# Order and fillers of block 0, and ten weight buffers from slot 22 of block 1, in a two-layer hybrid decoder step

## The chip, the cores and the metric

The kernel runs on one core of a Trainium2 chip. The metric is device time in microseconds, the median of three runs. Each core has a matrix engine (PE, with its weight loads as PEld), a vector engine (DVE), an activation engine (ACT), a general engine (POOL), and SP, which here only issues DMA transfers and waits. Each engine works through its own list of instructions in order, and an instruction may wait for semaphores that other engines or landed transfers raise. ACT issues the weight transfers from its own list; SP issues all others.

## The reference

Two layers over a prompt of 2048 tokens (width 1024) and over eight single decode tokens. Cut to what matters:

```python
h = _rmsnorm(x, norm_w)
z = einsum('btd,dc->btc', h, w_in)          # q,k,v,gate of GLA; 16 low-rank gate inputs; q,k,v,gate of retention
la = log_sigmoid(glr @ gla_w2 + gla_b) / 16
# GLA:       S_t = exp(la_t) S_{t-1} + k_t^T v_t ;  o_t = q_t S_t
# retention: S_t = gamma_h S_{t-1} + k_t^T v_t ;    o_t = q_t S_t   (q, k rotated)
o_a = rms(o_a) * silu(gate_a);  o_b = groupnorm(o_b) * silu(gate_b)
y = x + concat(o_a, o_b) @ w_out            # twice (DEPTH = 2); then a final RMSNorm
```

The outputs are both token streams and, per layer, the recurrent states of the prompt and of the eight decode rows.

## The kernel before, in words

The prompt is cut into four blocks of 512 tokens per layer, so there are eight block passes, n = 0 to 7; n = 0 to 3 are layer 0, n = 4 to 7 layer 1. "Block 0" and "block 1" are the first and second pass of a layer (`kind` 0 and 1). In a pass PE runs 32 slots (w = 1 to 32) and a slot 0. Four slots make a unit u, which fills the four accumulator banks P[0..3] over eight K tiles, two K tiles a slot. A slot holds 24 matmuls of 512 columns: four banks by two K tiles by three products (high by high, low by high, high by low part), since each fp32 operand is split into a high and a low part (`products`, L733). Slot 0 (`hT_slot0`, L700) multiplies the normed activations by the 16 low-rank gate columns; `gate_expand` (L754) turns that into the forget gate.

The weights of a slot are two halves h (512 columns each), 64 halves a pass. For each half ACT issues the load (`load_half`, L258) and makes the high part (`split_hi`, L267); POOL makes the low part (`split_lo`, L274), which PE awaits as `lo_done`. In its turn w, ACT does: split half 2w+2, load half 2w+4, split half 2w+3, load half 2w+5, and only then the copies of that turn. There are ten staging buffers: 0 to 3 are `w_stage`, 4 to 7 lie in `ss` and 8 to 9 in `v_b`. `ss` and `v_b` also hold the decode states and products, which block 1 needs. So `buffer(h)` gives block 1 only buffers 0 to 3 for its first halves, and all ten later. Before a load into a buffer, ACT waits until POOL has split the buffer's last half; where no half has used the buffer within the last ten, it waits for `state_out`: both decode states of the layer stored by SP (`save_states`, L466), and for the decode outputs (`so_ps`). `state_out` is 64 after layer 0 and 128 after layer 1.

SP's list in a pass follows w = 0 to 19. At w = 6 it turns the keys through DRAM (`out_k_rows` L437, `k_n` L442), at w = 16 to 19 of the passes n = 3 to 6 it reads the next block's activations with eight transfers each (`load_next`, L397), and at w = 19 of block 1 it stores the GLA decode state (L466), behind that turn's `load_next`.

At the start (n = 0) DVE computes row statistics, POOL the reciprocal roots, PE turns them into a bank (`scale_rows`, L364), DVE scales the K tiles one after the other (`next_scaled`, L377), ACT makes their high part (`next_hi`, L353), DVE their low part (`next_lo`, L357). Between these DVE works on the decode rows: `sample_stats`, `sample_mean`, `sample_norm`. In block 1, DVE and ACT in slots 20 to 25: `outputs_pair` (L994, L1000) is PE's attention output, ACT copies it (L1189), DVE takes its statistics (L1563), multiplies gates (`silu`, L1592) and normalises (L1586).

Of the kernel before, what the change touches and what calls it, by code (L numbers as in the profile page):

```python
# [25 lines left out]
TOK = 128  # L26
# [34 lines left out]
def build(nc, d):  # L61
# [3 lines left out]
    with ctx:  # L65
# [164 lines left out]
        def buffer(h):  # L230
            return h % HALVES % STAGED if h // HALVES % NBLK == 1 and h % HALVES < 48 else h % STAGES
# [126 lines left out]

        def scale_rows(pe):

            for t in range(TPB):
                if t % 2 == 0:
                    pe.wait_ge(first_rs, t // 2 + 1)
                i = pe.transpose(ATT[:, TOK * t:TOK * t + TOK], xrs[:, t:t + 1].to_broadcast([128, 128]), ident[:, :])  # L364
            i.then_inc(ht_ps.sem, KT)

# [226 lines left out]
        def _(pool):  # L593
# [36 lines left out]
            for h in range(2):  # L630
                split_lo(pool, h)
            pool.wait_ge(s_v.sem, s_v.at(0, V_NV - V_LAST))
            rsqrt(srs[:, :], svar[:, :], s_p.sem)
            for h in range(2, 2 * AHEAD):
                split_lo(pool, h)
# [41 lines left out]
        def _(pe):  # L677
# [10 lines left out]
            for l in range(DEPTH):  # L688
                def body(l, n, kind):
                    def hT_slot0():  # L690
# [11 lines left out]
                        if kind == 0 and n > 0:  # L702
# [55 lines left out]
                    def first_slot():  # L758

                        for k in range(2):  # L760
                            pe.wait_ge(lo_done, k + 1)
                            pe.wait_ge(hlo_sb.sem, hlo_sb.at(0, k + 1))
                            products(0, 0, 0, (k,))
                        for q in range(4):
                            if q > 0:
                                i = products(0, 0, q)
                            if q == 0:
# [3 lines left out]
                    def unit_slot(u, s):  # L771
                        first = n * HALVES + 2 * (4 * u + s)
# [7 lines left out]
                        for q in range(4):  # L780
# [3 lines left out]
                            if n == 0 and u == 0 and s == 1:  # L784
                                if q == 0:
                                    sample_transposed(0)
                                if q == 1:
                                    gate_expand()
                                if q == 2:
                                    sample_gate()  # L790
                            if q < 3 and s == 3:
                                i.then_inc(proj.sem, 1)
                        if kind == 0 and u < 6 and s % 2 == 1:
                            if s == 1:
                                free_sample_bank(u)
# [55 lines left out]
                    def sample_work(w):  # L851
                        if kind == 0:
                            if w == 2:
# [4 lines left out]
                            if w == 6:  # L858
# [157 lines left out]
                    for w in range(1, SLOTS):  # L1016
                        u, s = (w - 1) // 4, (w - 1) % 4
                        if n == 0 and w == 1:
                            first_slot()
                            hT_slot0()  # L1020
# [5 lines left out]
                        if w == 1:  # L1026
                            gate_expand()
                        if kind > 0:
# [27 lines left out]
        def _(act):  # L1056
# [7 lines left out]
            split_hi(act, 0)  # L1064
            split_hi(act, 1)
            load_half(act, 4)
            load_half(act, 5)
            for k in range(KT):
                next_hi(act, 0, k)
                if k in (3, 5):  # L1070
                    split_hi(act, (k + 1) // 2)
            for l in range(DEPTH):
                def body(l, n, kind):
# [11 lines left out]
                    def sample_work(w):  # L1085
# [7 lines left out]
                        if w == 2:  # L1093
# [830 lines left out]
```

## Time and profile before

| | |
|---|---|
| median of 3 runs | 1668.95 us (1668.67 to 1671.54) |
| the profiled execution | 1668.71 us, its span 1666.9 us |
| PE busy | 1641.7 us (98%) |
| DVE, ACT, POOL busy | 1064.9, 618.6, 840.0 us |
| granted clock of TensorE | 0.999 of full speed |

The span runs from the first to the last instruction; 1.8 us of the execution lie outside it. Times in the rows are microseconds from the span's start. A row of the timeline gives start, duration, engine, line of the kernel, operation, names, shape and count, and in brackets the idle time of the engine before it with what ended it. Consecutive matmuls overlap, so the cost of one is read from the distance between two starts, not from its duration.

### The profile page before, as it was taken

What the parts mean: (1) busy time and instruction counts of PE and PEld (TensorE: products, weight loads), DVE (VectorE), ACT (ScalarE), POOL (GpSimd) and SP (SyncE); (2) the same over time, 40 slices, a digit from 0 to 9 for tenths busy, and PEclk for the clock granted to TensorE, in tenths of its full rate; (3) what the DMA queues carried; (4) which work ended last, traced back from release to release, by engine and by line L of the source; (5) the groups of instructions that cost most, each with busy time, mean ns of one, the idle gap of its engine ahead of it and who ended that gap; (6) DMA issues with size and microseconds to landing.
All of it is one profiled execution on the core that took longest, in us unless ns stands there. A gap on an engine that the chain in (4) does not pass through costs nothing.

```text
span 1666.9 us, 26235 instructions
## 1 busy us (share of the span) xinstructions
PE 1641.7 (98%) x9742; PEld 1346.4 (81%) x9742; DVE 1064.9 (64%) x2388; ACT 618.6 (37%) x1166; POOL 840.0 (50%) x645
## 2 busy tenths in 40 slices
PE   6999999999999999999999999999999999999998
PEld 4788878887788887888878888788887888878886
DVE  7743666867765575547855467767787557784474
ACT  4423444243342343423443234342333424442342
POOL 4443645645455464444544445556554555554455
PEclk9999999999999999999999999999999999999999
DMA  7634657656564474467643566567864466553554
GB/s 266 154 109 110 183 203 221 192 155 169 194 177 128 114 208 133 120 151 160 202 134 97 151 143 196 163 172 188 193 193 132 122 163 158 171 173 103 142 155 142
DMA packets 389136, 268.19 MB, mean 161 GB/s; under 512 B 290704, under 2 KB 293136, under 8 KB 389008
## 3 DMA queue, kind: packets, MB, share of 16 engines
q1 hardware_dynamic: 315136, 131.99, 31.6%
q10 hardware_dynamic: 73872, 134.51, 25.6%
q8 instruction: 77, 1.26, 0.3%
q14 instruction: 51, 0.42, 0.1%
HBM read 219.34 MB, written 47.07 MB: 160 GB/s over the span
## 4 chain that ended last, share of the span: by engine, by line
PE 90%; DVE 4%; DMA 2%; issue 1%; SPq 1%; POOL 0%; ACT 0%; ACTq 0%; POOLq 0%; DVEq 0%
PE bank L733 78%; PE bank L994 2%; PE bank L1000 1%; PE bank L978 1%; PE bank L956 1%; PE bank L798 1%; PE bank L935 1%; SPq L442 1%; DMA region<-in_x_prompt 1%; PE bank L700 1%; DMA out_k_rows<-region 1%; DMA w_stage<-in_w_slots 1%; PE bank L939 1%; PE bank L1011 0%; PE bank L808 0%
## 5 line engine op out<-in xcount | busy, mean ns | idle before, releaser
L274 POOL TENSOR_TENSOR w_lo<-w_stage,w_hi 128x512 fp32r<-128x512 f32 x264 | 371.7, 1428 | 331.3 <-ACT w_hi L267 331.2
L733 PE MATMUL bank<-h_hi,w_hi 128*128 128x512 f32 x1024 | 408.3, 399 | 4.1 <-DVE h_lo L357 4.1
L733 PE MATMUL bank<-h_lo,w_hi 128*128 128x512 f32 x1024 | 399.8, 390 | 0.0
L733 PE MATMUL bank<-h_hi,w_lo 128*128 128x512 f32 x1024 | 399.4, 390 | 0.0
L274 POOL TENSOR_TENSOR w_lo<-ss,w_hi 128x512 fp32r<-128x512 f32 x164 | 224.3, 1387 | 211.2 <-ACT w_hi L267 211.1
L267 ACT ACTIVATE w_hi<-w_stage 128x512 fp32r<-128x512 f32 x264 | 153.8, 624 | 369.1 <-PE bank L733 286.8
L733 PEld LDWEIGHTS bank<-h_hi,w_hi 128*128 128x128 f32 x1024 | 192.4, 188 | 55.4 <-issue 8.1
L733 PEld LDWEIGHTS bank<-h_hi,w_lo 128*128 128x128 f32 x1024 | 192.5, 188 | 41.1
L733 PEld LDWEIGHTS bank<-h_lo,w_hi 128*128 128x128 f32 x1024 | 192.7, 188 | 37.2
L733 PE MATMUL bank<-w_hi,m_hi 128*128 128x512 f32 x512 | 200.6, 392 | 2.0 <-DVE region L1592 2.0
L733 PE MATMUL bank<-w_hi,h_hi 128*128 128x512 f32 x512 | 201.1, 393 | 0.0
L733 PE MATMUL bank<-w_lo,h_hi 128*128 128x512 f32 x512 | 199.4, 389 | 0.0
L733 PE MATMUL bank<-w_lo,m_hi 128*128 128x512 f32 x512 | 199.3, 389 | 0.0
L733 PE MATMUL bank<-w_hi,h_lo 128*128 128x512 f32 x512 | 199.2, 389 | 0.0
L733 PE MATMUL bank<-w_hi,m_lo 128*128 128x512 f32 x512 | 199.2, 389 | 0.0
L267 ACT ACTIVATE w_hi<-ss 128x512 fp32r<-128x512 f32 x164 | 95.8, 624 | 232.0 <-PE bank L733 176.6
L274 POOL TENSOR_TENSOR w_lo<-v_b,w_hi 128x512 fp32r<-128x512 f32 x84 | 115.9, 1399 | 116.2 <-ACT w_hi L267 116.0
L607 POOL TENSOR_TENSOR rstd<-var,half 128x4 f32<-128x4 f32 x64 | 66.7, 1042 | 128.9 <-DVE var L1576 68.0
L733 PEld LDWEIGHTS bank<-w_hi,m_hi 128*128 128x128 f32 x512 | 96.1, 188 | 24.2 <-issue 4.3
L733 PEld LDWEIGHTS bank<-w_hi,h_hi 128*128 128x128 f32 x512 | 96.2, 188 | 21.5 <-issue 1.2
L733 PEld LDWEIGHTS bank<-w_hi,m_lo 128*128 128x128 f32 x512 | 96.1, 188 | 20.2
L733 PEld LDWEIGHTS bank<-w_hi,h_lo 128*128 128x128 f32 x512 | 96.1, 188 | 20.2
(218 smaller groups left out, 2209.9 us busy)
## 6 DMA issues: line engine op xcount, KB each, us to landing
w_stage<-in_w_slots ACTq DMA_DIRECT2D x264, 256.0 KB, 3.7
ss<-in_w_slots ACTq DMA_DIRECT2D x164, 256.0 KB, 3.6
v_b<-in_w_slots ACTq DMA_DIRECT2D x84, 256.0 KB, 3.7
region<-in_x_prompt SPq DMA_DIRECT2D x32, 512.0 KB, 5.2
out_o_rows<-region SPq DMA_DIRECT2D x64, 256.0 KB, 3.1
region<-out_o_rows SPq DMA_DIRECT2D x192, 64.0 KB, 3.4
xn<-in_x_t SPq DMA_DIRECT2D x16, 512.0 KB, 5.0
out_k_rows<-region SPq DMA_DIRECT2D x32, 256.0 KB, 3.9
```

The lines of the kernel that those rows point to most:

```text
L267: nc.scalar.activation(w_hi[:, h // 2 % RING, c], stage(h), ACT.Copy).then_inc(hi_done, 1)
L274: pool.tensor_tensor(w_lo[:, r, c], stage(h), w_hi[:, r, c].bitcast(f32), ALU.subtract).then_inc(lo_done, 1)
L442: sp.dma_start(k_n[32 * j:32 * j + 32, t, :].rearrange("p (f a) -> p f a", a=32), runs[t][j]).then_inc(kb_in.sem, 16)
L607: pool.tensor_tensor(dst, src, half[0:dst.shape[0], 0:dst.shape[-1]], ALU.pow).then_inc(s, 1)
L700: i = pe.matmul(ATT[r, 0:256], wg[:, k, :], x_t[:, k, 256 * hf:256 * hf + 256], start=(k < 2), stop=(k >= 6))
L733: i = pe.matmul(P[q][:, :], x, y, start=(s == 0 and kk == 0 and c == 0), stop=(s == 3 and kk == 1 and c == 2), skip_group_check=True)
L798: i = pe.matmul((ST if Z_BANK[u] == "S" else X)[32 * c:32 * c + 32, 0:128], hs[:, k, :], stage(first - 2 * s + k)[:, 128 * c:128 * c + 128 ...
L935: pe.matmul(OUT[hh][:, c], a[:, h, :], v_n[:, t, 128 * h:128 * h + 128], start=(p == 0), stop=False, skip_group_check=True)
L939: i = pe.matmul(OUT[hh][:, c], q_two[g][r, p, tile], s[r, c], start=False, stop=(p == 1), skip_group_check=True)
L956: i = pe.matmul((ST, X)[t // 2][r, c:c + 128], k_n[:, t, 64 * h:64 * h + 64], v_n[:, t, 128 * h:128 * h + 128], start=True, stop=True)
L978: i = pe.matmul(SC_TWO[hh][:, c:c + 128], k_t[r, p, tile], q_two[g][r, p, tile], start=True, stop=True)
L994: pe.matmul(OUT_TWO[hh][:, c:c + 128], a_two[g][:, t % 2, h, :], v_n[:, t, 128 * h:128 * h + 128], start=(t % 2 == 0 and p == 0), stop=Fal ...
```

## The change

In block 0 of the first pass (n = 0): slot 0's low-rank product moves from behind slot 1 to behind slot 2; the decode rows' transposes, gate and gate expansion move later by one place or one slot, and ACT and DVE follow (`late`). `idle_turns` puts 10, 18 and 8 transposes of the identity into an unread bank on PE: between the two pairs of `scale_rows`, behind them, and between the products of the first and the second K tile. `sample_norm` stands two K tiles sooner on DVE. ACT makes the high part of K tile 0 ahead of weight half 1. POOL splits halves 2 and 3 before the decode root. On DVE `queries` is taken out of `rotate`; it stands in front of the second half of the gate. In both layers, block 1 uses all ten buffers from half 42 (slot 22) instead of half 48 (slot 25).

```diff
         def buffer(h):
-            return h % HALVES % STAGED if h // HALVES % NBLK == 1 and h % HALVES < 48 else h % STAGES
+            return h % HALVES % STAGED if h // HALVES % NBLK == 1 and h % HALVES < 42 else h % STAGES
...
+        def idle_turns(pe, count):
+
+            for _ in range(count):
+                pe.transpose(X[:, 0:128], ident[:, :], ident[:, :])
+
         def scale_rows(pe):
             for t in range(TPB):
                 if t % 2 == 0:
+                    if t > 0:
+                        idle_turns(pe, 10)
                     pe.wait_ge(first_rs, t // 2 + 1)
                 i = pe.transpose(ATT[:, TOK * t:TOK * t + TOK], xrs[:, t:t + 1].to_broadcast([128, 128]), ident[:, :])
             i.then_inc(ht_ps.sem, KT)
+            idle_turns(pe, 18)
...
             for h in range(2):
                 split_lo(pool, h)
+            for h in range(2, 2 * AHEAD):
+                split_lo(pool, h)
             pool.wait_ge(s_v.sem, s_v.at(0, V_NV - V_LAST))
             rsqrt(srs[:, :], svar[:, :], s_p.sem)
-            for h in range(2, 2 * AHEAD):
-                split_lo(pool, h)
...
                             products(0, 0, 0, (k,))
+                            if k == 0:
+                                idle_turns(pe, 8)
                         for q in range(4):
                             if q > 0:
                                 i = products(0, 0, q)
-                            if q == 0:
+                            if q == 2:
                                 sample_sum(0)
...
-                            if n == 0 and u == 0 and s == 1:
-                                if q == 0:
-                                    sample_transposed(0)
-                                if q == 1:
-                                    gate_expand()
-                                if q == 2:
-                                    sample_gate()
+                            if n == 0 and w == 2 and q == 2:
+                                sample_transposed(0)
+                            if n == 0 and w == 3 and q == 0:
+                                gate_expand()
...
                             if s == 1:
+                                if u == 0:
+                                    pe.wait_ge(s_v.sem, s_v.at(l, V_H))
                                 free_sample_bank(u)
...
                             first_slot()
-                            hT_slot0()
                             continue
...
+                        if n == 0 and w == 2:
+                            hT_slot0()
...
             split_hi(act, 0)
+            next_hi(act, 0, 0)
             split_hi(act, 1)
-            load_half(act, 4)
-            load_half(act, 5)
-            for k in range(KT):
+            for k in range(1, KT):
                 next_hi(act, 0, k)
-                if k in (3, 5):
-                    split_hi(act, (k + 1) // 2)
+                if k == 1:
+                    load_half(act, 4)
+                    load_half(act, 5)
+                if k in (2, 3):
+                    split_hi(act, k)
...
-                if k == 7:
+                if k == 5:
                     sample_norm(0)
-            vec.wait_ge(const_in, 96)
-            vec.tensor_scalar(gmask[:, :], rmask[:, 0:TOK], 0.0, None, ALU.is_gt)
...
+                        if w == 5:
+                            queries()
+                        if kind == 0 and w == 4 + late:
+                            sample_gate()
-                        if w in (3, 4):
-                            hf = w - 3
+                        if w in (3 + late, 4 + late):
+                            hf = w - 3 - late
```

What this makes of the lists shows at three places. First, PE's list at the start of the first pass, from the first wait for the second pair of roots to the decode sum. Before:

```order
L364 MATMUL bank<-ident,xrs 128x128 [waits first_rs]
L364 MATMUL bank<-ident,xrs 128x128
L733 MATMUL bank<-h_hi,w_hi 128x512 [waits hlo_sb,lo_done]
L733 MATMUL bank<-h_lo,w_hi 128x512
L733 MATMUL bank<-h_hi,w_lo 128x512
L733 MATMUL bank<-h_hi,w_hi 128x512 [waits hlo_sb,lo_done]
L733 MATMUL bank<-h_lo,w_hi 128x512
L733 MATMUL bank<-h_hi,w_lo 128x512
L685 MATMUL bank<-sms,gsum 128x2 [waits s_v,first_in]
```

and now, from the second transpose of the first pair to the end of K tile 1 of bank 0:

```order
L371 MATMUL bank<-ident,xrs 128x128
L362 MATMUL bank<-ident 128x128 x10
L371 MATMUL bank<-ident,xrs 128x128 [waits first_rs]
L371 MATMUL bank<-ident,xrs 128x128
L362 MATMUL bank<-ident 128x128 x18
L741 MATMUL bank<-h_hi,w_hi 128x512 [waits hlo_sb,lo_done]
L741 MATMUL bank<-h_lo,w_hi 128x512
L741 MATMUL bank<-h_hi,w_lo 128x512
L362 MATMUL bank<-ident 128x128 x8
L741 MATMUL bank<-h_hi,w_hi 128x512 [waits hlo_sb,lo_done]
L741 MATMUL bank<-h_lo,w_hi 128x512
L741 MATMUL bank<-h_hi,w_lo 128x512
```

Transposes of the identity (`bank<-ident`, 10, 18 and 8) stand before the second pair, behind it, and between the two K tiles; the decode sum (`gsum`) has moved out of these rows to behind bank 2.

Second, DVE's list in slots 3 to 5 of the first pass: `la` is the log gate, `nb` its offset, `al` the decode gate, and `qdec` rows are `queries`. Before:

```order
L1662 SCALAR_TENSOR_TENSOR la<-bank,tmp 128x2x256 [waits o_ps,gate_l]
L1666 SCALAR_TENSOR_TENSOR la<-keep,la 128x256 [waits la_sb]
L1666 SCALAR_TENSOR_TENSOR la<-keep,la 128x256
L1670 TENSOR_SCALAR nb<-la 128x2x2 [waits scan_sb]
L1670 TENSOR_SCALAR nb<-la 128x2x2
L1662 SCALAR_TENSOR_TENSOR la<-bank,tmp 128x2x256 [waits o_ps,gate_l]
L1666 SCALAR_TENSOR_TENSOR la<-keep,la 128x256 [waits la_sb]
L1666 SCALAR_TENSOR_TENSOR la<-keep,la 128x256
L1670 TENSOR_SCALAR nb<-la 128x2x2 [waits scan_sb]
L1670 TENSOR_SCALAR nb<-la 128x2x2
L1304 SCALAR_TENSOR_TENSOR al<-bank,gt 128x16 [waits gl_s]
L1630 TENSOR_TENSOR region<-bank,qdec 128x512 [waits stored,proj]
L1630 TENSOR_TENSOR region<-bank,qdec 128x512 [waits proj]
```

and now:

```order
L1683 SCALAR_TENSOR_TENSOR la<-bank,tmp 128x2x256 [waits o_ps,gate_l]
L1687 SCALAR_TENSOR_TENSOR la<-keep,la 128x256 [waits la_sb]
L1687 SCALAR_TENSOR_TENSOR la<-keep,la 128x256
L1691 TENSOR_SCALAR nb<-la 128x2x2 [waits scan_sb]
L1691 TENSOR_SCALAR nb<-la 128x2x2
L1641 TENSOR_TENSOR region<-bank,qdec 128x512 [waits stored,proj]
L1641 TENSOR_TENSOR region<-bank,qdec 128x512 [waits proj]
L1317 SCALAR_TENSOR_TENSOR al<-bank,gt 128x16 [waits gl_s]
L1683 SCALAR_TENSOR_TENSOR la<-bank,tmp 128x2x256 [waits o_ps,gate_l]
L1687 SCALAR_TENSOR_TENSOR la<-keep,la 128x256 [waits la_sb]
L1687 SCALAR_TENSOR_TENSOR la<-keep,la 128x256
L1691 TENSOR_SCALAR nb<-la 128x2x2 [waits scan_sb]
```

`queries` and the decode gate, which waits for ACT (`gl_s`), now stand ahead of the second half of the gate (`bank,tmp`); the rotation follows this piece in both.

Third, ACT's list in turn 20 and the start of turn 21 of block 1 in layer 1 (n = 5): the splits of halves 42 and 43, the loads of halves 44 and 45 behind each, and the copies that follow. Before:

```order
L267 ACTIVATE w_hi<-w_stage 128x512 [waits slot_used,w_loaded2]
L258 DMA w_stage<-in_w_slots 128x512 [waits lo_done]
L267 ACTIVATE w_hi<-w_stage 128x512 [waits w_loaded3]
L258 DMA w_stage<-in_w_slots 128x512 [waits lo_done]
L1189 ACTIVATE region<-bank 128x4x128 [waits o_ps,or_out]
L1189 ACTIVATE region<-bank 128x4x128
L1143 ACTIVATE region<-bank 128x512 [waits proj,s_v]
L1143 ACTIVATE region<-bank 128x512 [waits proj] x2
L1143 ACTIVATE region<-bank 128x512 [waits slot_used]
L267 ACTIVATE w_hi<-w_stage 128x512 [waits slot_used,w_loaded0]
```

and now:

```order
L267 ACTIVATE w_hi<-w_stage 128x512 [waits slot_used,w_loaded2]
L258 DMA ss<-in_w_slots 128x512 [waits so_ps,state_out]
L267 ACTIVATE w_hi<-w_stage 128x512 [waits w_loaded3]
L258 DMA ss<-in_w_slots 128x512 [waits so_ps,state_out]
L1204 ACTIVATE region<-bank 128x4x128 [waits o_ps,or_out]
L1204 ACTIVATE region<-bank 128x4x128
L1158 ACTIVATE region<-bank 128x512 [waits proj,s_v]
L1158 ACTIVATE region<-bank 128x512 [waits proj] x2
L1158 ACTIVATE region<-bank 128x512 [waits slot_used]
L267 ACTIVATE w_hi<-ss 128x512 [waits slot_used,w_loaded0]
```

The two loads go to `ss` in place of `w_stage`, and wait for `state_out` in place of `lo_done`. The rest of the list stands as before.

## Rows read from the trace of the kernel before

**Rows 1.** The page, busy time by engine.

```profile
PE 1641.7 (98%) x9742; PEld 1346.4 (81%) x9742; DVE 1064.9 (64%) x2388; ACT 618.6 (37%) x1166; POOL 840.0 (50%) x645
```

**Rows 2.** Waits of PE: in total, times, longest.

```profile
PE bank L733 <- DVE h_lo L357: 4.1, 1, 4.1
PE bank L733 <- DVE region L1592: 2.0, 1, 2.0
```

**Rows 3.** Timeline of PE, the start: start, duration, what.

```profile
8.70 0.66 PE L364 MATMUL bank<-ident,xrs 128*128 128x128 f32 x2 [8.70 <-POOL xrs L607]
11.61 0.69 PE L364 MATMUL bank<-ident,xrs 128*128 128x128 f32 x2 [2.26 <-POOL xrs L607]
16.35 0.77 PE L733 MATMUL bank<-h_hi,w_hi 128*128 128x512 f32 x1 [4.05 <-DVE h_lo L357]
...
17.77 0.63 PE L733 MATMUL bank<-h_hi,w_hi 128*128 128x512 f32 x1
...
19.71 0.40 PE L733 MATMUL bank<-h_lo,w_hi 128*128 128x512 f32 x1
...
23.38 0.39 PE L733 MATMUL bank<-h_hi,w_lo 128*128 128x512 f32 x1
24.67 1.93 PE L700 MATMUL bank<-xn,wg 128*32 128x256 f32 x32 [0.90 <-DVE xn L377]
```

**Rows 4.** Timeline of DVE, first pass.

```profile
15.09 1.12 DVE L357 TENSOR_TENSOR h_lo<-xn,h_hi 128x512 fp32r<-128x512 f32 x1 [1.27 <-ACT h_hi L353]
```

**Rows 5.** Chain that ended last, the stretch with the keys.

```profile
46.71 1.18 DVE region L1630 x2
54.95 6.88 DMA out_k_rows<-region
79.48 1.16 PE bank L935 x8
```

**Rows 6.** Timeline of four engines, block 1 of layer 0.

```profile
379.84 0.63 ACT L267 ACTIVATE w_hi<-w_stage 128x512 fp32r<-128x512 f32 x1 [1.87 <-POOL w_lo L274]
...
387.97 1.14 ACT L1208 ACTIVATE m_hi<-region 128x512 fp32r<-128x512 f32 x2
...
389.66 3.28 DVE L1619 TENSOR_TENSOR m_lo<-tmp,m_hi 128x512 fp32r<-128x512 f32 x2 [6.21 <-ACT m_hi L1208]
...
396.44 0.47 PE L733 MATMUL bank<-w_hi,m_hi 128*128 128x512 f32 x1 [1.96 <-DVE region L1592]
```

**Rows 7.** Tile `out_gla_s`, in layer 0 and then in layer 1.

```profile
L466 SPq DMA_DIRECT2D out_gla_s<-ss x2: 431/460/488, 350.1 to 350.6; - x2
...
DMA to landing us min/median/max: 3.9/4.2/4.5
...
L466 SPq DMA_DIRECT2D out_gla_s<-ss x2: 432/464/495, 1189.8 to 1190.3; - x2
...
DMA to landing us min/median/max: 5.7/6.8/7.8
```

**Rows 8.** Timeline of SP and ACT, block 1 of layer 1.

```profile
1169.01 20.75 SPq L397 DMA_DIRECT2D xn<-out_acts  x32
...
1180.31 0.82 ACTq L258 DMA_DIRECT2D w_stage<-in_w_slots  x2
...
1183.17 1.09 ACT L1189 ACTIVATE region<-bank 128x512 f32<-128x512 f32 x2 [1.74 <-PE bank L1000]
```

**Rows 9.** Timeline of DVE and PE, block 1 of layer 1.

```profile
1185.33 0.86 DVE L1563 BATCH_NORM_STATS2 bns<-region 128x6 f32<-128x128 f32 x4
1188.51 2.47 DVE L1592 SCALAR_TENSOR_TENSOR region<-region,bank 128x512 f32<-128x512 f32 x4
...
1213.79 1.88 DVE L1592 SCALAR_TENSOR_TENSOR region<-region,bank 128x512 f32<-128x512 f32 x3
...
1189.46 1.95 PE L994 MATMUL bank<-region,la 128*128 128x128 f32 x16
...
1215.26 0.39 PE L733 MATMUL bank<-w_hi,m_hi 128*128 128x512 f32 x1
```

More of the change, by code:

```diff
@@ L701, in hT_slot0 @@
                         i.then_inc(slot_used, 1)
-                        if kind == 0 and n > 0:
+                        if kind == 0:
                             sample_gate()
@@ L771, in unit_slot @@
                     def unit_slot(u, s):
+                        w = 4 * u + s + 1
                         first = n * HALVES + 2 * (4 * u + s)
@@ L852, in sample_work @@
                         if kind == 0:
-                            if w == 2:
+                            if w == 2 + int(n == 0):
                                 pe.wait_ge(lrs_sb.sem, lrs_sb.at(l, 1))
@@ L857, in sample_work @@
                                 i.then_inc(gx_ps.sem, 1)
-                            if w == 6:
+                            if w == 6 + int(n == 0):
+                                pe.wait_ge(s_v.sem, s_v.at(l, V_LA))
                                 z_transposed(X[:, 256:384], 0)
@@ L1092, in sample_work @@
                             return
-                        if w == 2:
+                        if w == 2 + late:
                             act.wait_ge(lrs_ps.sem, lrs_ps.at(l, 1))
                             nc.scalar.activation(lr_s[0:RANK, :], X[0:RANK, 128:136], ACT.Copy).then_inc(lrs_sb.sem, 1)
-                        if w == 3:
+                        if w == 3 + late:
                             act.wait_ge(gx_ps.sem, gx_ps.at(l, 1))
@@ L1102, in sample_work @@
                             nc.scalar.activation(gt[:, :], gt[:, :], ACT.Ln, bias=1.0).then_inc(gl_s.sem, 1)
-                        if w in (7, 14, 22, 26):
-                            c = (7, 14, 22, 26).index(w)
+                        if w in (7 + late, 14, 22, 26):
+                            c = (7 + late, 14, 22, 26).index(w)
                             col = (0, 8, 4, 12)[c]
@@ L1116, in sample_work @@
                                                      ACT.Tanh, scale=0.5).then_inc(tg_s.sem, 1)
+                    late = int(n == 0)
                     for w in range(SLOTS):
-                        if w == (1 if n > 0 else 2):
-                            act.wait_ge(slot_used, n * SLOTS + (1 if n > 0 else 2) + RING)
+                        if w == (1 if n > 0 else 3):
+                            act.wait_ge(slot_used, n * SLOTS + w + RING)
                             act.wait_ge(const_in, 96)
@@ L1153, in body @@
                         sample_work(w)
-                        if w == 2:
+                        if w == 2 + late:
                             for hf, src in ((0, ATT), (1, OB)):
@@ L1423, in sample_work @@
                         if kind == 0:
-                            if w == 4:
-                                sample_gate()
                             if w == 8:
@@ L1619, in mixed_rest_ret, with queries @@
                         vec.tensor_tensor(m_lo[:, 4 + h, :], ret_t[h], m_hi[:, 4 + h, :].bitcast(f32), ALU.subtract).then_inc(mlo_sb.sem, 1)
-                    def rotate():
+                    def queries():
                         for p in range(2):
@@ L1630, in rotate @@
                             vec.tensor_tensor(q4[0], q4[1], qdec[:, p, :].unsqueeze(1).to_broadcast([128, TPB, TOK]), ALU.mult).then_inc(q_raw.sem, 1)
+                    def rotate():
                         vec.wait_ge(rope_in.sem, rope_in.at(n, 16))
@@ L1650, in rotate @@
                             c += 4
+                    late = int(n == 0)
                     if n == 0:
                         sample_start(l)
+                        vec.wait_ge(const_in, 96)
+                        vec.tensor_scalar(gmask[:, :], rmask[:, 0:TOK], 0.0, None, ALU.is_gt)
                     for w in range(1, SLOTS):
```

## The prediction

> **What bounds the kernel now.** I read the page first. PE is busy for 1641.7 of 1666.9 us [rows 1], so nearly everything that the other engines do lies beside PE, and a change can gain only where PE stands still or works slowly. The waits of PE come next: besides the reciprocal roots at the very start there is 4.1 us for the first low part of the activations and 2.0 us for a gate product [rows 2]. Then the timeline of the start [rows 3]. PE does four transposes, waits until 16.35, and its products start 0.43 to 0.56 us apart (16.35 to 17.77 is three of them). Later they start 0.23 us apart (19.71 to 23.38 is sixteen, 3.67 us). That is half speed, 1.2 against 2.4 GHz, though the granted clock of the whole run reads 0.999; PE was nearly idle before 16.35 and had worked without a break for about 3 us when it became fast. At 24.67 the low-rank product waited 0.90 us for the last scaled K tile. The reader is to see that the front holds some 3 us, block 1 of layer 0 holds 2 us, and nothing else holds any. So the largest question is whether the change makes a new wait in the 1640 us that are full.
>
> The sum is made against the profiled execution: span 1666.9, execution 1668.71 us, which is 0.24 below the median of 1668.95.
>
> **The front, on PE.** The low part of K tile 0 waited 1.27 us for ACT's high part [rows 4]; ACT now makes that part ahead of weight half 1, so it comes about 1.2 us sooner and PE's first product moves from 16.35 to about 15.1. Ten transposes at 0.23 us (the distance of two in the pair at 8.70, 0.66 for both with the last one's tail [rows 3]) fit between 9.1 and 11.61. The other 18 start at 12.1 and end at 16.2 if PE stays slow, at 14.1 if it turns fast about 3 us after 8.7, as it did after 16.35. If fast, the six products of K tiles 0 and 1 in bank 0 and the eight transposes end near 17.4 (K tile 1 is ready at about 16.3), and the remaining 18 products and the decode sum take 4.3 us: slot 1 ends at 21.7. Before it ended at 23.6 (23.38 plus 0.23). Gain 1.9 us. The low-rank product no longer stands in front of slot 2, where it waited: between 23.6 and 24.67 lies 1.06 us, all gained, since DVE has the eighth K tile by about 25 and PE comes to that product only at 28.5. Its own 1.9 us, the decode transposes, the gate expansion and the decode gate are the same instructions in another place, cost no more, and cancel. The POOL splits of halves 2 and 3 come before the root and end near 20.4, before slot 2 starts. Sum of the front on PE: 3.0 us by slot 5.
>
> **What keeps this from the end.** PE meets the keys' chain at 79.48: the rotation ends, `out_k_rows` is issued at 54.95 and lands 6.88 us later, 16 transfers bring the keys back, DVE scales them and finishes the first scores, and only then PE's L935 starts [rows 5]. The changed DVE list has the decode gate, with ACT's two table loads behind it, in front of the second half of the gate, and everything on ACT for the gate waits for the low-rank product, now at 30 instead of 26.5. I reckon ACT's last log at 39.8, the decode gate at 44.3 and the rotation's start at 46.8, against 47.9 (46.71 plus the 1.18 of `queries`, which goes ahead). So the rotation moves by 1.1 us only. The write of the keys then meets fewer transfers: the one at 54.95 landed late because an activation tile and two weight halves were issued within the microsecond before, and these move up with PE by 3 us. The bounds of the front are 1.0 us (landing unchanged) and 3.5 us (chain quicker than PE, the wait at L935 gone). I take 2.8.
>
> At this place one rule speaks against the change. No row before shows whether transposes raise the clock: the four in rows 3 are too few. The Trainium skill, "TensorE: Matmul & The Clock Gate", Part 4, says that full clock does not engage for transposes, which do not count as work in the same way. By the sum above PE then stays slow to its products: that is the first rival below, worked out from the distances in rows 3.
>
> **Block 1, layer 0.** PE stood 1.96 us at 396.44 [rows 2, 6]. ACT was held by POOL in front of half 47's split at 379.84, because half 48's load goes to the buffer that half 46 had just used; the four high parts at 387.97 came late, hence the low parts at 389.66, the decode work behind them, and the gate product for slot 25 [rows 6]. With ten buffers from half 42 the last use is at least six halves back, and POOL does not hold ACT. PE's 2.0 us go (none to 2.1). The new wait there is small. The loads of halves 42 and 43, issued at about 353.9, now wait for `state_out`; the state is stored at 350.1 and 350.6 and lands after at most 4.5 us, 355.1 [rows 7]. ACT loses 1.2 us in a turn where it is otherwise waiting for PE.
>
> **Block 1, layer 1, the term that decides.** Here half 44 is the first whose buffer (`ss`) has no recent user, so ACT waits for `state_out` of 128 at its load in turn 20, in place of the load issued at 1180.31 [rows 8]. But SP stores this layer's GLA state only behind its 32 transfers for the next block's activations, issued from 1169.01 to 1189.76 [rows 8]; the store goes out at 1189.8 and 1190.3, and the second part lands 7.8 us after issue, at 1198.1 [rows 7]. ACT works in order: rows 6 show that a held load holds the split behind it. So ACT stands from 1180.7 until the state is out. Queued behind are the split of half 43, a load, and the copies of the attention output, before at 1183.17 [rows 8]. PE's next `outputs_pair` (1189.46) overwrites what they read, and DVE's statistics (1185.33) read what they write [rows 9].
>
> How long? The landing at 1198.1 had two weight halves beside it that now wait too. The lower bound is layer 0's 4.5 us, giving 1194.9; the upper 1198.1. I take 1196.5, nearer the row of this very place, since the activation transfers are still there. The copies end 2.0 us after release (issue 0.4, split 0.5, two copies 1.1): 1198.5. PE then stood for 9 us. But DVE carries more: from 1185.33 to the gate product at 1213.79 it has no idle time [rows 9], so all of this moves by 1198.5 - 1185.3 = 13.2. The gate product ends 0.66 after its start, at 1214.45; PE's slot 25 started at 1215.26 [rows 9], so 0.8 is slack, less 0.1 for the hand-over: slot 25 starts 12.5 us later. The bounds are 10.9 (landing 1194.9) and 14.1 (landing 1198.1). PE's own delay up to there is 10 us (slot 21 waits for its first gate product, 1188.51 plus 0.66 plus 13.2 = 1202.4, against 1192.4, which is 1189.46 plus 1.95 and one more us for the second half of `outputs_pair`), below DVE's, and so slow matmuls after PE's idle time, at most 3 us of half speed that cost 1.5, lie under it too. After slot 25 every engine is late by about the same, and PE is full again; nothing gives it back.
>
> **Sum.** 1668.71 - 2.8 (front) - 2.0 (layer 0) + 12.5 (layer 1) = 1676.4 us. Its own range, from the bounds: 1668.7 - 3.5 - 2.1 + 10.9 = 1674.0 to 1668.7 - 1.0 - 0 + 14.1 = 1681.8.
>
> **Rivals.** First, PE stays slow through the transposes. Eighteen end at 16.2, three products cost 1.3, eight transposes 1.8, three products 1.3: 20.6, and then 18 products, the first three or four still slow, so slot 1 ends near 25.6, 2.0 later than before in place of 1.9 earlier. Less the wait of 1.06 the front is 0.9 slower; the sum is 1668.7 + 0.9 - 2.0 + 12.5 = 1680.1. For it speaks only that no row shows fast transposes after idle time; against it, that the transposes leave PE no gap either: one starts every 0.23 us. Chance 0.25.
>
> Second, on the other side: the state is out in time, or ACT is not held where it hurts. If the store reached the memory before 1180.7, or DVE's statistics did not need the copies, the layer 1 term is zero: 1668.7 - 2.8 - 2.0 = 1663.9, faster by 0.3%. For it speaks that the same wait in layer 0 costs ACT 1.2 us and PE nothing. Against it speak rows 7 and 8: SP's store is 9 us after ACT comes to the wait, and nothing in the change moves SP's list there. It decides from a landing at about 1183, where the copies stood. Chance 0.08.
>
> Third, the layer 1 stall is there but half as dear: DVE's work behind it runs faster, because POOL and the transfers stand still too, and PE bounds slot 25: the term is 8 us and the time 1671.9. Chance 0.07.
>
> The rest, 0.60, is the forecast.
>
> **How the numbers follow.** The likeliest is 1676.4. The forecast and the first rival hold 0.85 and reach from 1674.0 to about 1683; the third adds 1671.9. A range from 1672.0 to 1682.0 leaves out the second rival and the far end of the first. A measurement of this kernel can tell 0.2% (3.3 us) from no change, so slower starts at 1672.3: the forecast, the first rival and a third of the third, 0.87. Same: the rest of the third and some of the second, 0.06. Faster: 0.07.
>
> **What would show each step.** The start: products 0.23 us apart from the first, slot 1's end at 21.7. The keys: rotation's start at 46.8, L935 at 76.7. Layer 0: no wait of PE for the gate product near 391. Layer 1: an idle time of ACT of about 16 us before a split (L267) in block 1, released by the store of the state; a wait of PE of about 9 us in `outputs_pair` (L994 before), and a second wait of 2 to 3 us at slot 25 for the gate product. The prediction is wrong if ACT has no such idle time, or if slots 21 to 25 of layer 1 take back what the first wait cost.

## The result, and the profile after

| | before | after |
|---|---|---|
| median | 1668.9 us (6 runs, 1668.67 to 1671.54) | 1676.06 us (6 runs, 1674.95 to 1676.46) |
| ratio to before, 95% interval | | 1.0038 [1.0025, 1.0051] |
| profiled execution, span | 1668.71, 1666.9 | 1676.39, 1674.6 |
| granted clock | 0.999 | 0.995 |

The changed kernel is 0.4% slower; 1676.4 was forecast. PE's busy time on the page answers to [rows 1]: 7 us more, with 36 transposes more and as many products.

```profile
PE 1648.6 (98%) x9778; PEld 1354.1 (81%) x9778; DVE 1063.5 (64%) x2388; ACT 617.3 (37%) x1166; POOL 832.3 (50%) x645
```

The waits of PE, to be read beside [rows 2]. The columns are total, times, longest. The two old waits are gone; one of 7.7 us in the attention output has come (L1005 is L994 of before), and two of 0.9.

```profile
PE bank L371 <- POOL xrs L615: 8.7, 1, 8.7
PE bank L1005 <- ACT region L1204: 7.7, 1, 7.7
PE bank L967 <- DVE k_n L1483: 1.2, 2, 0.9
PE bank L741 <- DVE region L1603: 0.9, 1, 0.9
```

The start, PE's timeline, against [rows 3]. Eighteen transposes take 3.18 us, where ten before them took 2.34: they get faster on the way, 0.21 us apart up to the eleventh, which starts at 14.26, and 0.11 us apart from there. The products are 0.23 us apart from the second on (15.37 to 15.60), and slot 1's last starts at 21.51.

```profile
9.17 2.34 PE L362 MATMUL bank<-ident 128*128 128x128 f32 x10
...
12.12 3.18 PE L362 MATMUL bank<-ident 128*128 128x128 f32 x18
15.06 0.47 PE L741 MATMUL bank<-h_hi,w_hi 128*128 128x512 f32 x1
15.37 0.39 PE L741 MATMUL bank<-h_lo,w_hi 128*128 128x512 f32 x1
15.60 0.39 PE L741 MATMUL bank<-h_hi,w_lo 128*128 128x512 f32 x1
...
21.51 0.40 PE L741 MATMUL bank<-h_hi,w_lo 128*128 128x512 f32 x1
22.15 0.51 PE L741 MATMUL bank<-h_hi,w_hi 128*128 128x512 f32 x1 [0.24 <-POOL w_lo L274]
```

The key turn, timelines of DVE, SP and PE, against [rows 5]. Queries (L1641), the rotation's first row, the two writes of the keys, the reads back behind them, and PE's L946, which was L935 at 79.48.

```profile
44.00 1.28 DVE L1641 TENSOR_TENSOR region<-bank,qdec 128x512 f32<-128x512 f32 x2
...
48.45 0.74 DVE L1657 STREAM_SHUFFLE tmp<-region 128x512 f32<-128x512 f32 x1
...
51.77 5.05 SPq L445 DMA_DIRECT2D out_k_rows<-region  x2
58.68 8.06 SPq L450 DMA_DIRECT2D k_n<-out_k_rows  x16
...
76.23 1.05 PE L946 MATMUL bank<-region,tmp 128*128 128x128 f32 x8
```

Block 1 of layer 0, ACT's timeline, against [rows 6]: the split behind `w_stage` waits for PE, no longer for POOL, and the load into `ss` at 351.63 did not wait at all. The high parts of `m` come at 381.94 (387.97 before).

```profile
351.55 0.63 ACT L267 ACTIVATE w_hi<-w_stage 128x512 fp32r<-128x512 f32 x1 [7.51 <-PE bank L741]
351.63 0.33 ACTq L258 DMA_DIRECT2D ss<-in_w_slots  x1
...
381.94 1.14 ACT L1223 ACTIVATE m_hi<-region 128x512 fp32r<-128x512 f32 x2
```

Block 1 of layer 1, ACT, then SP with the landings of its store, DVE and PE, against [rows 7, 8, 9].

```profile
1191.67 0.63 ACT L267 ACTIVATE w_hi<-w_stage 128x512 fp32r<-128x512 f32 x1 [14.67 <-DMA out_gla_s<-ss]
...
1192.21 1.08 ACT L1204 ACTIVATE region<-bank 128x512 f32<-128x512 f32 x2
...
1168.30 18.64 SPq L405 DMA_DIRECT2D xn<-out_acts  x32
1186.98 0.96 SPq L474 DMA_DIRECT2D out_gla_s<-ss  x2
...
L474 SPq DMA_DIRECT2D out_gla_s<-ss x2: 432/460/487, 1187.0 to 1187.5; - x2
...
DMA to landing us min/median/max: 3.0/3.4/3.8
...
1193.33 0.87 DVE L1574 BATCH_NORM_STATS2 bns<-region 128x6 f32<-128x128 f32 x4 [11.81 <-ACT region L1204]
...
1193.44 3.75 PE L1005 MATMUL bank<-region,la 128*128 128x128 f32 x16 [7.73 <-ACT region L1204]
...
1222.87 0.47 PE L741 MATMUL bank<-w_hi,m_hi 128*128 128x512 f32 x1 [0.94 <-DVE region L1603]
```

This is one chain. SP issues 32 transfers and only then the store; ACT stands 14.67 us in front of a split, until the store lands; the copies follow at 1192.21, DVE's statistics at 1193.33, PE's `outputs_pair` at 1193.44, and slot 25's gate product waits again.

Where PE's products stand against before is worked out from their starts in both traces:

| place | before | after | shift |
|---|---|---|---|
| n = 0, slot 1 | 16.35 | 15.06 | -1.3 |
| n = 0, slot 10 | 82.69 | 79.33 | -3.4 |
| n = 1, slot 10 | 291.99 | 289.64 | -2.4 |
| n = 1, slot 25 | 396.44 | 391.97 | -4.5 |
| n = 5, slot 21 | 1192.43 | 1198.94 | +6.5 |
| n = 5, slot 25 | 1215.26 | 1222.87 | +7.6 |
| end of the span | 1666.89 | 1674.57 | +7.7 |

### The profile page after: what moved, and what is told of

Same layout as the page of the kernel before. It is cut to its first block, busy times and chain, and to the rows that moved or that the text cites. A ratio compares the mean times of both kernels' runs of the same rounds, so it can differ in the third digit from the quotient of the medians.

```text
span 1674.6 us, 26307 instructions
## 1 busy us (share of the span) xinstructions
PE 1648.6 (98%) x9778; PEld 1354.1 (81%) x9778; DVE 1063.5 (64%) x2388; ACT 617.3 (37%) x1166; POOL 832.3 (50%) x645
## 4 chain that ended last, share of the span: by engine, by line
PE 89%; DVE 4%; SPq 3%; DMA 3%; issue 1%; ACT 0%; POOL 0%; ACTq 0%; POOLq 0%; DVEq 0%
PE bank L741 76%; PE bank L1005 2%; PE bank L1011 1%; SPq L450 1%; PE bank L808 1%; PE bank L989 1%; PE bank L967 1%; DMA out_k_rows<-region 1%; SPq L405 1%; PE bank L946 1%; PE bank L708 1%; SPq L437 1%; PE bank L950 1%; PE bank L762 1%; PE bank L1022 0%
## 5 line engine op out<-in xcount | busy, mean ns | idle before, releaser
L274 POOL TENSOR_TENSOR w_lo<-w_stage,w_hi 128x512 fp32r<-128x512 f32 x256 | 355.5, 1409 | 343.7 <-ACT w_hi L267 343.4
L274 POOL TENSOR_TENSOR w_lo<-ss,w_hi 128x512 fp32r<-128x512 f32 x170 | 229.6, 1371 | 228.9 <-ACT w_hi L267 228.8
L267 ACT ACTIVATE w_hi<-w_stage 128x512 fp32r<-128x512 f32 x256 | 148.5, 624 | 374.3 <-PE bank L741 297.0
```

The lines of the kernel that those rows point to most:

```text
L267: nc.scalar.activation(w_hi[:, h // 2 % RING, c], stage(h), ACT.Copy).then_inc(hi_done, 1)
L274: pool.tensor_tensor(w_lo[:, r, c], stage(h), w_hi[:, r, c].bitcast(f32), ALU.subtract).then_inc(lo_done, 1)
```

## The experiments

Each was timed beside the kernel before, whose median was 1669.45, 1669.98 or 1669.24 us from one set of executions to the next, so ratios are compared rather than medians of different sets. "The variant" below is the first. "Own pace" means a kernel's shift against before just ahead of the place in question; where a trace is compared, it is that of one execution.

**Layer 0 alone gets the early ten buffers.**

```diff
-... and h % HALVES < 42 else h % STAGES
+... and h % HALVES < (42 if h < NBLK * HALVES else 48) else h % STAGES
```

> The changed kernel, but layer 1 keeps buffers 0 to 3 up to half 48; only layer 0 goes over at half 42. My theory: the whole loss is ACT's wait for the stored state in turn 20 of block 1 of layer 1, so 11.6 us go (from -3.97 before it to +7.62 behind it in the profile): about 1664.5 us, ratio to before 0.997. No wait of PE for the copies, none at slot 25 of layer 1. Rival A (the loss comes from the reordered start as it reaches layer 1): unchanged near 1676. Rival B (only half is that wait, the rest PE's slow clock for some other reason): near 1670.

Measured 1663.91 us (1663.56 to 1664.28), ratio 0.9967 [0.9954, 0.9979]. The whole loss is gone; PE's only waits in this trace are the one at the very start, which the load of the identity ends here, and 0.2 us for a weight half of slot 2:

```profile
PE bank L371 <- DMA ident<-in_ident: 9.1, 1, 9.1
```

Slot 25 of n = 5 starts at 1210.81, 12.1 us before the changed kernel's. The variant is faster than both kernels, by 0.33% against before.

**The buffers alone**, on the kernel before, in both layers.

```diff
-... and h % HALVES < 48 else h % STAGES
+... and h % HALVES < 42 else h % STAGES
```

> The kernel before with nothing but ten buffers from half 42 in both layers. My theory: layer 0 gains 2.0 us, layer 1 loses 11.6, perhaps 12 since nothing has been moved up by the start: 1668.9 + 9.8 = 1678.7 us. Rival (the loss needs the moved start): no slower than 1669.

Measured 1677.55 us (1677.19 to 1678.31), ratio 1.0049 [1.0035, 1.0063]. The loss needs nothing from the start. ACT shows the same stall, 1.9 us shorter: it comes to it 3.4 us later (1180.4 against 1177.0), and the state lands 1.5 us later.

```profile
1193.23 0.63 ACT L267 ACTIVATE w_hi<-w_stage 128x512 fp32r<-128x512 f32 x1 [12.79 <-DMA out_gla_s<-ss]
```

In the shifts of its trace layer 0 gives 2.1 us (from +0.2 to -1.9), of which 1.5 are lost again at the end of n = 3, and slot 25 of n = 5 is 9.0 us late, 9.5 against its own pace. I had expected 11.6 to 12 for layer 1: that left out that without the changed start ACT comes to the wait later, by more than SP to the store.

**All buffers early, and the store first.** In layer 1 the state store moves in SP's list from behind the 32 transfers to in front of them.

```diff
+                    if b == 1 and w == (16 if l else 19):
+                        sp.wait_ge(s_v.sem, s_v.at(l, V_SS[1]))
+                        save_states(l, "gla_s")
                     if w >= 16 and NBLK - 1 <= n < LAST:
                         load_next(n + 1, w - 16)
...
-                        if w == 19:
-                            sp.wait_ge(s_v.sem, s_v.at(l, V_SS[1]))
-                            save_states(l, "gla_s")
```

> The changed kernel with all ten buffers from half 42 in both layers, but in layer 1 SP stores the GLA decode state in front of its 32 transfers for the next block's activations (turn 16) instead of behind them. My theory: the state is out some 15 us before ACT comes to the wait, so the 11.6 us go although the buffers stay: 1664.5 us, within 0.5 us of the kernel whose layer 1 keeps four buffers. The activations come about 1 us later, which nobody waits for. Rival A (ten buffers themselves cost, through earlier weight loads that meet the other transfers): stays above 1670. Rival B (the activation transfers, now behind the store, become late for DVE's turn 23): between, 1666 to 1668.

Measured 1664.33 us (1663.42 to 1664.75), ratio 0.9969 [0.9957, 0.9982]. Here ACT has all ten buffers in layer 1 as well, and no wait: the state has landed at 1170.9 (4.8 us behind its second issue), 5 us before the load, where I had expected some 15 (SP, then ACT):

```profile
1165.06 2.06 SPq L474 DMA_DIRECT2D out_gla_s<-ss  x2
1167.17 20.07 SPq L405 DMA_DIRECT2D xn<-out_acts  x32
...
1176.07 0.34 ACTq L258 DMA_DIRECT2D ss<-in_w_slots  x1
1176.53 0.61 ACT L267 ACTIVATE w_hi<-w_stage 128x512 fp32r<-128x512 f32 x1
```

So the buffer rule by itself costs nothing; the place of one store behind 32 transfers does. It also shows that layer 1 gains nothing from the early buffers: PE's shift is -4.3 us ahead of slot 21 and at slot 25.

**A dose of the same: the store ahead of the last eight transfers**, in the same turn (w = 19), so behind 24 of the 32.

```diff
+                    if b == 1 and w == 19:
+                        sp.wait_ge(s_v.sem, s_v.at(l, V_SS[1]))
+                        save_states(l, "gla_s")
                     if w >= 16 and NBLK - 1 <= n < LAST:
...
```

> The changed kernel with one move in SP's list: in both layers the store of the GLA state stands ahead of the eight activation transfers of turn 19, in place of behind them. Theory (ACT is held until the store lands, and all behind it moves by as much): 24 of 32 transfers stand in front of the store, so it is issued 8 x 0.58 = 4.7 us sooner, lands 3.8 us behind its second issue as in the changed kernel, ACT's idle time in front of half 43's split is 10.0 us in place of 14.7, PE's slot 25 of layer 1 is 11.6 - 4.7 = 6.9 us late, and the time is 1676.1 - 4.7 = 1671.4. Rival (PE's own work bounds slots 21 to 25 once the wait is short): down to 1669.

Measured 1671.82 us (1670.09 to 1672.77, 11 runs), ratio 1.0015 [1.0005, 1.0024]. The stall and PE's two waits, from ACT's timeline and PE's waits:

```profile
1186.55 0.63 ACT L267 ACTIVATE w_hi<-w_stage 128x512 fp32r<-128x512 f32 x1 [9.79 <-DMA out_gla_s<-ss]
...
PE bank L1005 <- ACT region L1204: 2.9, 1, 2.9
PE bank L741 <- DVE region L1603: 1.6, 1, 1.6
```

Slot 25 of n = 5 goes from 4.2 us early to 2.4 us late, 6.5 where I had expected 6.9. The store's second issue comes 5.2 us sooner than in the changed kernel (1182.3 for 1187.5), ACT's stall is 4.9 shorter, slot 25 has 5.0 less of delay: what the store gains, the end gains, one for one. The rival, that PE's own work sets a floor, is out at this size.

**Layer 1 from half 46**: the held load comes one turn later.

```diff
+... and h % HALVES < (42 if h < NBLK * HALVES else 46) else h % STAGES
```

> The changed kernel, with layer 1 going over to ten buffers at half 46: ACT comes to the wait one turn later, at about 1185.6 us instead of 1176.4. My theory: the wait ends at the same 1191.3 and holds ACT for 5.6 us; the copies of turn 21 come 3 us late, DVE's slack of 0.8 is taken off, so 2.1 us of the 11.6 remain: 1666.6 us. PE waits for no copies. Rival A (any wait there costs the same): 1676. Rival B (only the first wait counts, this one is hidden): 1664.5.

Measured 1668.06 us (1665.94 to 1672.85, 11 runs), ratio 0.9993 [0.9984, 1.0002]: not told from before, and 0.26% above the variant's ratio, some 4.3 us. ACT stands 5.80 us, and slot 25 of n = 5 is 3.8 us late against its own pace (from +0.3 to +4.1); I had expected 2.1. The direction holds and the size is nearly twice mine. What I had left out stands in PE's waits: the transposes of the decode outputs in front of slot 24 (L858) waited for DVE as well.

```profile
PE bank L858 <- DVE o_s L1413: 2.2, 1, 2.2
PE bank L741 <- DVE region L1603: 1.3, 1, 1.3
```

The profiled execution, 1672.85, is the slowest of the 11; it lost another 4.9 us in block 1 of layer 0, which the last section takes up.

**The start alone**: both layers keep half 48.

```diff
+... and h % HALVES < 48 else h % STAGES
```

> The changes at the start alone: both layers keep the ten buffers from half 48, as before. Theory (start -3.4, layer 0 of block 1 -2.0, and no term of layer 1): the wait of PE for the gate product near slot 25 of both first blocks is back as in the kernel before, slot 25 of n = 1 starts 2 us later than in the variant that keeps half 48 in layer 1 alone, and the time is 1663.9 + 2.0 = 1665.9. Rival (the buffers of layer 0 gave nothing, the start gave all): 1663.9.

Measured 1666.42 us (1665.24 to 1671.67, 11 runs), ratio 0.9982 [0.9973, 0.9991]. PE's wait for the gate product is back, in n = 1 alone as in the kernel before (I had named n = 5 as well), and slot 25 of n = 1 starts at 393.71 where the variant has it at 391.76:

```profile
393.71 0.47 PE L741 MATMUL bank<-w_hi,m_hi 128*128 128x512 f32 x1 [1.90 <-DVE region L1603]
```

So layer 0's buffers are worth 1.9 to 2.5 us and the start 2.3 (its profiled execution against before's) to 3.6 (the medians, against 1669.98).

**The variant without the 36 transposes.**

```diff
-                        idle_turns(pe, 10)
-            idle_turns(pe, 18)
-                                idle_turns(pe, 8)
```

> The variant that keeps half 48 in layer 1, with all 36 unread transposes of the start left out. Theory (the transposes raise the clock, but PE's saving is bounded by when DVE delivers K tiles): the first product starts at about 14.9, products are 0.43 apart for about 3 us and slot 1 ends near 22.3 instead of 21.7; 0.5 to 0.9 us longer than with them, 1664.4 to 1664.8. Rival one (the transposes give all of what PE gained in slot 1): 1.9 us longer, 1665.8. Rival two (they do nothing, the clock would have risen anyway): 1663.9.

Measured 1664.78 us (1663.48 to 1665.6), ratio 0.9965 [0.9953, 0.9977]. By time alone this can't be told from the variant. The trace tells it: the eleven products from 15.59 on are slow, in the main 0.43 us apart, and slot 2 starts at 23.97, against 22.74.

```profile
15.59 0.77 PE L741 MATMUL bank<-h_hi,w_hi 128*128 128x512 f32 x1 [3.09 <-DVE h_lo L357]
...
17.28 0.77 PE L741 MATMUL bank<-h_hi,w_hi 128*128 128x512 f32 x1
17.84 0.63 PE L741 MATMUL bank<-h_lo,w_hi 128*128 128x512 f32 x1
18.27 0.63 PE L741 MATMUL bank<-h_hi,w_lo 128*128 128x512 f32 x1
...
20.75 0.39 PE L741 MATMUL bank<-h_hi,w_lo 128*128 128x512 f32 x1
```

The transposes are worth 1.2 us at slot 2, and 0.9 of it is left at slot 10 and 0.7 at the end of layer 0. The two profiled executions (1665.60 and 1664.28) are 1.3 apart, but that holds a wait of 0.8 us in n = 3 (at 816.22, for DVE) that the variant's trace has not. My 22.3 for slot 1's end was too early by 1.7: PE was slow for 4.8 us (15.59 to 20.40), with a gap in front of K tile 1 at 17.28, and not for the 3 us that I had carried over from [rows 3]. All 36 give less than the 1.9 of the first rival there.

**Fewer transposes**: 14 in place of 18, none between the K tiles.

```diff
-            idle_turns(pe, 18)
+            idle_turns(pe, 14)
...
-                            if k == 0:
-                                idle_turns(pe, 8)
```

> The variant that keeps half 48 in layer 1, with 14 instead of 18 transposes behind the roots' and none between K tiles 0 and 1. Theory (the last transposes already stand in the way of the first product, whose operand is ready at 14.65, and 14 raise the clock as well): the first product starts at 14.9 in place of 15.1 to 15.5, products are 0.23 apart; PE waits for K tile 1 up to 0.6 us and the clock stays high over so short a gap; 0 to 0.4 us less than 1663.9. Rival (the gap at K tile 1 lets the clock fall, or 14 are too few): half speed for some products, 0.5 us or more longer.

Measured 1664.27 us (1663.51 to 1664.95), ratio 0.9963 [0.9951, 0.9975]: the same as the variant. PE now stands 0.68 and 0.77 us, and its products stay 0.23 apart behind both gaps:

```profile
15.23 0.47 PE L741 MATMUL bank<-h_hi,w_hi 128*128 128x512 f32 x1 [0.68 <-DVE h_lo L357]
...
16.92 0.47 PE L741 MATMUL bank<-h_hi,w_hi 128*128 128x512 f32 x1 [0.77 <-DVE h_lo L357]
17.23 0.39 PE L741 MATMUL bank<-h_lo,w_hi 128*128 128x512 f32 x1
17.46 0.39 PE L741 MATMUL bank<-h_hi,w_lo 128*128 128x512 f32 x1
```

The rival, a clock that falls in the gap, is out for gaps this short. The eight transposes between the K tiles and the last four of the 18 do nothing that the time shows.

**Transposes and ACT's order on the kernel before**; the low-rank product stays behind slot 1. ACT's order is taken over whole: besides the high part of K tile 0, the loads of halves 4 and 5 and the splits of halves 2 and 3 stand where the changed kernel has them.

```diff
+                        idle_turns(pe, 10)
+            idle_turns(pe, 18)
+                                idle_turns(pe, 8)
...
             split_hi(act, 0)
+            next_hi(act, 0, 0)
             split_hi(act, 1)
-            load_half(act, 4)
-            load_half(act, 5)
-            for k in range(KT):
+            for k in range(1, KT):
                 next_hi(act, 0, k)
-                if k in (3, 5):
-                    split_hi(act, (k + 1) // 2)
+                if k == 1:
+                    load_half(act, 4)
+                    load_half(act, 5)
+                if k in (2, 3):
+                    split_hi(act, k)
```

> The kernel before with the 36 transposes and ACT's high part of K tile 0 ahead of weight half 1, and nothing else: the low-rank product stays behind slot 1. Theory (the two bring slot 1's end from 23.6 to 21.7 to 22.0, but the low-rank product then waits for the eighth K tile, which DVE still delivers near 24.6): PE waits 2.5 us or so in slot 0's product, slot 2 starts at 26.3 to 26.6 as before, and the time is that of the kernel before, 1669 +-1. Rival (each part of the start pays its own share): 1.9 us less than before, 1667.

Measured 1667.38 us (1666.44 to 1669.46, 12 runs), ratio 0.9983 [0.9975, 0.9992]. My theory fell: the time is 2.6 us under before (1.7 between the profiled executions), where it expected none. The eighth K tile did not stay near 24.6:

```profile
23.76 1.93 PE L708 MATMUL bank<-xn,wg 128*32 128x256 f32 x32 [1.51 <-DVE xn L385]
25.62 0.50 PE L741 MATMUL bank<-h_hi,w_hi 128*128 128x512 f32 x1
```

Against [rows 3] the low-rank product starts 0.91 us sooner. DVE makes scaled tiles and low parts in one list, so the 1.27 us that it no longer waits for K tile 0 [rows 4] move the whole list: its eighth scaled tile starts at 22.97, where before it was 23.88. Half of my argument held: the product does wait, 1.51 us, and where it stands behind slot 2, as in the variant, no trace shows that wait.

These two parts give most of what the start gives: slot 10 of n = 0 is 1.7 us early here and 2.9 in the start alone, and the two medians are 1.0 apart, with overlapping ratios. How the rest divides among the product's place, DVE's order and POOL's order no run tells.

## Why the prediction was right

The total was right and so was its mechanism. Several sizes were off, partly against each other.

**Layer 1, +12.5.** Each link is in the rows: ACT's wait before a split, its release by the store of the state, the late copies, the statistics, `outputs_pair`, the second wait at slot 25. The term measured 11.5 us against the kernel's own pace (from -3.9 at slot 20 of n = 5 to +7.6 at slot 25). Two of its sizes were off, and against each other. I took 6.2 us from the store's second issue to its landing, nearer this place's own 7.8 [rows 7]; it was 3.8, below my lower bound of 4.5. 7.8 had been measured with weight loads beside it that the stall itself held back, and the other traces bear this out: 3.8 to 4.0 us in the four with the stall, 5.0 to 7.8 in the six where the store stands in its old place and the loads run on. That is 2.4 us less. On the other side I had let SP's list move up with PE; PE came to this place 3.9 us sooner and the store's second issue only 2.8, which is 1.1 more. DVE's list behind the stall took 0.3 longer. The store ahead of the last eight transfers confirmed the one-for-one dependence, and the store first that nothing else in the rule costs anything.

**What hid the slow clock.** I allowed 3 us of half speed behind PE's wait, costing 1.5 at most. By the granted clock it was half speed for 10 us:

```profile
1185.70:1188.40 2.70, 0.01 (x1) 1.00 0.85 153
1188.50:1198.60 10.10, 5.16 (x30) 0.50 0.54 194
1198.70:1205.00 6.30, 6.30 (x35) 1.00 0.22 83
```

(A stretch, its length, PE's busy time and matmuls, granted clock, DMA share, GB/s.) PE had stopped at 1185.7. The 32 matmuls of `outputs_pair` took 3.75 + 1.89 us, against 1.95 [rows 9] and one: 2.7 us more. Slot 21 is 10.4 us late against its own pace, where I had 10. It cost nothing at the end, because DVE's list was the longer one: slot 25 still waited 0.94 us. So of the two waits that I named, 9 us and 2 to 3, there came 7.73 and 0.94, and the slow matmuls filled what lay between: 7.7 + 2.7 + 0.9 is 11.3 of the 11.5.

**The front, -2.8.** Slot 1 ended at 21.7, as worked out. POOL's splits ended at 22.1 and not at 20.4, so PE waited 0.24 us in front of slot 2, and slot 5 came 2.7 sooner where I had 3.0. Behind it one step was wrong, and another made good for it. I had the rotation start at 46.8; it starts at 48.45, later than the 47.88 of before, since DVE came to the queries only at 44.0 and the second half of the gate stands between them and the rotation. The second write of the keys is then issued at 56.5, 1.6 later than before, but it lands in 2.2 us in place of 6.9, and the reads back follow at 58.68, while before they followed at 61.8 [rows 5]. That was near my upper bound, 3.5: slot 10 shows 3.4. That a reckoned gain on DVE turned into a loss and a landing made good for it is luck. One microsecond of it was lost in block 1 (below), so 2.4 reached n = 1, slot 10.

**Block 1 of layer 0, -2.0.** From -2.4 to -4.5: 2.1. The loss of 1.2 us on ACT did not come: the second part of the state was issued at 346.1 in place of 350.6 and had landed at 351.2. In five of the other traces ACT did stand there, for 0.4 to 2.2 us, and PE did not wait.

**The first rival, slow transposes, is refuted.** The pace of the transposes rises within the 18, and the products behind them are fast from the start, while without them eleven are slow. The Trainium skill, "TensorE: Matmul & The Clock Gate", Part 4, says that full clock does not engage for a transpose in transpose mode; the fp32 transposes of this kernel, which the trace shows as matmuls with the identity, did raise it (0.21 us apart, then 0.11). The rows do not name their mode. By time alone the gain from them can't be told: the two ratios are 0.9965 and 0.9967.

**The sum.** -3.4 + 1.0 (lost in n = 1) - 2.1 + 0.6 (0.3 in n = 2, 0.3 at the end of n = 3) + 11.5 = +7.6, against +7.7 forecast. The closeness of the two is partly luck: the layer 1 term was 1.0 too high and the others together 0.9 too low.

## What to carry to other kernels

When a buffer rule is relaxed, ask at the first new use which event frees the buffer, and where that event's instruction stands in its own queue: a store behind 32 transfers held a load, the load held copies, and 14.7 us of idle ACT became 11.5 at the end. Moving the store was as good as taking the rule back. At a start where the first operands come late, work that nobody reads can raise the clock, but it pays only for as much as the operands' own chain allows: 1.2 us at slot 2 here, and 24 transposes gave as much as 36.

## What the runs showed of the hardware that was not expected

**The slow clock outlasted the pause.** PE stood for 7.7 us. The granted clock read full for the first part of that, half from 1188.44 to 1198.68, and the 5.2 us of work in that stretch ran at half speed. In the other traces PE's waits of 2.9 us (store ahead of the last eight), 3.2 us (from half 46, in n = 1) and 5.9 us (buffers alone) were followed by half speed for 3.4, 3.4 and 6.8 us. Waits of 1.9 to 2.2 us (1.96 before at 396.44, 1.90 in the start alone, 2.19 from half 46) left it at full, and gaps of 0.7 to 0.9 us at the start left the products' pace unchanged.

**At the start the view of the clock misleads.** It reads 1.00 in stretches where products are 0.43 us apart. With the stretch's columns as above, the variant without transposes:

```profile
18.00:19.00 1.00, 1.00 (x4) 1.00 1.11 366
```

But this trace's list of granted-clock stretches begins only at 20.64 us, and the view counts time without an entry as full. The first entry lies where the distances change: at 20.64 here (0.23 us apart from 20.75 on), at 19.48 in the kernel before (from 19.71), at 14.26 in the changed kernel, within the 18 transposes. In the eight traces with transposes it lies between 11.97 and 15.04, in the three without between 19.48 and 21.41. So the record does date the rise, and a mean such as 0.999 counts the slow start as full.

**Block 1's key turn is a second edge.** In n = 1 PE comes to L967 just when the keys are back. With PE pulled forward there is a wait of 0.90 us in the changed kernel, none in the variant, and 3.20 in the profiled execution from half 46:

```profile
286.65 1.97 PE L967 MATMUL bank<-region,k_n 128*64 128x128 f32 x32 [0.90 <-DVE k_n L1483]
```

```profile
272.50 9.24 SPq L450 DMA_DIRECT2D k_n<-out_k_rows  x16
...
289.62 3.40 PE L967 MATMUL bank<-region,k_n 128*64 128x128 f32 x32 [3.20 <-DVE k_n L1483]
```

SP took 9.24 us for the 16 reads there, 9.04 in the changed kernel, 8.82 in the variant and 7.85 in before, and the slowest landed after 4.9, 4.5, 3.6 and 3.7 us. The 4.9 us that this execution lost are the 3.20 of the wait and 1.7 at half speed behind it. That would explain executions 4 to 5 us above their median, but no run changed this turn by itself, so it stays open.
